# x taken transposed from the host as well: projections of the unnormalised x, the row scale rstd applied behind them

## The reference, cut to what matters

```python
def _rms_norm(x, gain):
    y = x * lax.rsqrt(jnp.mean(x * x, axis=-1, keepdims=True) + EPS)
    return y * gain

h = _rms_norm(x, norm_mix[l])
proj = h @ w_in[l]                                   # 1024 x 3072
q, k, v, cb, cc, cu = jnp.split(proj, splits, axis=-1)
q = _rms_norm(q.reshape(b, s, 8, 64), q_norm[l])     # k alike with k_norm
attn = stick_breaking_attention(q, k, v)             # strictly causal, 8 heads
conv = cb * causal_conv_width_3(cc * cu, conv_w[l])
x = x + concat([attn, conv]) @ w_out[l]
h = _rms_norm(x, norm_ffn[l])
x = x + (silu(h @ w_gate[l]) * (h @ w_up[l])) @ w_down[l]
```

## Time and profile before

| what | value |
|---|---|
| median of 3 runs | 2436.81 us (2435.79 to 2438.77) |
| the profiled execution | 2439.77 us, its span 2438.0 us, granted clock 0.999 |
| TensorE matmuls busy | 2405.6 us, 99% of the span |
| VectorE | 1456.5 us, 60% |
| ScalarE | 1165.8 us, 48% |
| GpSimd | 1240.2 us, 51% |
| DMA | 388.07 MB, mean 159 GB/s |

### The profile page before, as it was taken

The page is one execution under the profiler, slowest core; times in us unless marked ns, Lnnn a source line. Parts: engine busy times, 40 slices in busy tenths (PEclk is TensorE's granted clock), DMA queues, the critical chain, the costliest instruction groups (busy, mean ns, idle before and its releaser), DMA issues.

```text
span 2438.0 us, 33295 instructions
## 1 busy us (share of the span) xinstructions
PE 2405.6 (99%) x11880; PEld 2015.0 (83%) x11880; DVE 1456.5 (60%) x1499; ACT 1165.8 (48%) x1866; POOL 1240.2 (51%) x880
## 2 busy tenths in 40 slices
PE   8999999999999999999999999999999999999999
PEld 6888878888888888888888888888878888888887
DVE  4444377787777777436755555556645555554555
ACT  4322277788777777323533333334533333333333
POOL 1455367878787877104754544306755545440021
PEclk9999999999999999999999999999999999999999
DMA  6989874443634641534333233386743232325665
GB/s 199 312 286 289 253 222 108 143 113 101 176 84 120 175 132 54 172 130 165 124 112 125 78 116 110 124 291 224 230 150 110 88 125 78 116 95 193 223 218 199
DMA packets 337503, 388.07 MB, mean 159 GB/s; under 512 B 21472, under 2 KB 242784, under 8 KB 335072
## 3 DMA queue, kind: packets, MB, share of 16 engines
q1 hardware_dynamic: 337376, 386.49, 50.3%
HBM read 263.20 MB, written 123.21 MB: 158 GB/s over the span
## 4 chain that ended last, share of the span: by engine, by line
PE 90%; DVE 2%; DMA 2%; SPq 2%; issue 2%; ACT 1%; POOL 1%; ACTq 0%; DVEq 0%; POOLq 0%
PE lay_ps L2582 11%; PE lay_ps L2584 11%; PE lay_ps L2586 11%; PE lay_ps L106 8%; PE lay_ps L107 8%; PE lay_ps L108 8%; PE lay_ps L2612 5%; PE lay_ps L2613 5%; PE lay_ps L2614 5%; PE lay_ps L1381 5%; PE lay_ps L1369 2%; PE lay_ps L1388 2%; PE lay_ps L1368 2%; PE lay_ps L1387 2%; POOL lay_A L2486 1%
## 5 line engine op out<-in xcount | busy, mean ns | idle before, releaser
L2486 POOL TENSOR_TENSOR lay_A<-lay_raw,lay_A 128x512 fp32r<-128x512 f32 x264 | 365.0, 1395 | 376.1 <-ACT lay_A L2101 375.9
L2582 PE MATMUL lay_ps<-lay_B,lay_A 128*128 128x512 f32 x1232 | 479.6, 389 | 0.4 <-DVE lay_B_over L1741 0.2
L2584 PE MATMUL lay_ps<-lay_B,lay_A 128*128 128x512 f32 x1232 | 479.3, 389 | 0.0
L2586 PE MATMUL lay_ps<-lay_B,lay_A 128*128 128x512 f32 x1232 | 479.3, 389 | 0.0
L1288 POOL TENSOR_TENSOR lay_a<-lay_a,lay_stick 128x128 f32<-128x128 f32 (+5 forms) x192 | 282.4, 1478 | 105.1 <-DVE lay_stick L1229 48.3
L2351 DVE TENSOR_TENSOR lay_A<-lay_A_over,lay_A 128x1024 fp32r<-128x1024 f32 x154 | 215.9, 1403 | 163.9 <-ACT lay_A L2145 163.5
L2101 ACT ACTIVATE lay_A<-lay_raw 128x512 fp32r<-128x512 f32 x264 | 162.0, 627 | 282.9 <-DMA lay_raw<-in_w_gate 110.2
L2145 ACT ACTIVATE lay_A<-lay_A_over 128x1024 fp32r<-128x1024 f32 x154 | 163.1, 1060 | 242.5 <-PE lay_ps L2614 214.5
L2582 PEld LDWEIGHTS lay_ps<-lay_B,lay_A 128*128 128x128 f32 x1232 | 231.3, 188 | 49.3 <-POOL lay_A L2486 1.0
L2586 PEld LDWEIGHTS lay_ps<-lay_B,lay_A 128*128 128x128 f32 x1232 | 231.3, 188 | 47.9
L2584 PEld LDWEIGHTS lay_ps<-lay_B,lay_A 128*128 128x128 f32 x1232 | 231.3, 188 | 47.8
(11 more groups left out here) (145 smaller groups left out, 4979.5 us busy)
## 6 DMA issues: line engine op xcount, KB each, us to landing
hid_ops<-lay_s SPq DMA_DIRECT2D x154, 256.0 KB, 2.0
lay_A_over<-hid_ops SPq DMA_DIRECT2D x154, 256.0 KB, 2.8
lay_w_stage<-in_w_in SPq DMA_DIRECT2D x48, 512.0 KB, 4.8
lay_raw<-in_w_gate SPq DMA_DIRECT2D x22, 1024.0 KB, 5.6
lay_raw<-in_w_up SPq DMA_DIRECT2D x22, 1024.0 KB, 8.1
lay_A_over<-wd_ops SPq DMA_DIRECT2D x88, 256.0 KB, 3.0
lay_A_over<-in_w_down SPq DMA_DIRECT2D x66, 256.0 KB, 4.6
lay_wd_raw<-in_w_down SPq DMA_DIRECT2D x11, 1024.0 KB, 6.8
```

The costliest lines, as they stand in the source:

```text
L2486: nc.gpsimd.tensor_tensor(A[:, j, p, 1, :, :], operand(j, p), A[:, j, p, 0, :, :].bitcast(F32), ALU.subtract).then_inc(lo_done, 1)
L2582: nc.tensor.matmul(ps[:, b, :], A[:, j, p, 0, k, :], B[p][:, 0, k, :], start=first_mm, stop=False, skip_group_check=True)
L2584: nc.tensor.matmul(ps[:, b, :], A[:, j, p, 0, k, :], B[p][:, 1, k, :], start=False, stop=False, skip_group_check=True)
L2586: mm = nc.tensor.matmul(ps[:, b, :], A[:, j, p, 1, k, :], B[p][:, 0, k, :], start=False, stop=last_mm, skip_group_check=True)
```

## The change

The host hands over three more arrays, made by transposing alone: `x_columns` (x transposed, 1024 by 2048), `x_tiles` (the same, tile by tile, so that a tile is one contiguous 512 KB block) and `mix_gain` (the gain as 128 by 8, 4 KB). Since the row scale rstd of a token multiplies a whole row of h, it is left out of the projections' operand and put in afterwards.

- **Opening.** `x_transpose`, `x_norm` and both hT stores go. SyncE loads `x_tiles` (`load_xT`, 512 KB) beside the rows of x, which still serve `x_square`. VectorE multiplies the two halves by the gain in place (`gain_part`), ScalarE rounds (`hT_part`), VectorE makes the remainder, both now from SBUF. The order of the w_in thirds, of x and of xT at the start is new. The last two k steps of tiles 0 and 1 are done tile by tile. All loops over tiles are written out. rstd is used in the split of v (ScalarE with a scale, VectorE scalar_tensor_tensor). q and k are normalised per head, so their rstd falls out except beside eps: GpSimd makes eps_x = eps * msq and adds that in place of eps. SyncE stores rstd (`store_r`, 512 bytes).
- **Attention.** Row i of pair p is loaded raw from `x_columns` (`load_raw`, one DMA of 256 KB, 5 buffers), ScalarE multiplies by the gain and rounds (`row_hi`), VectorE makes the remainder (`row_lo`). The tables ROW_LOADS, ROW_HI and ROW_LO place them: five loads in units 8 to 17 of the pair before, three in 46 and 47; the splits behind the work of units 45 and 47 and of units 0 to 2 of the pair itself, on VectorE behind the scan of the unit. NU is 48, and n + NU is unit n of the pair itself. For the first pair five rows are loaded at tile 6 and split within tile 15, three follow the last q/k split. rstd of the 512 tokens is read as a broadcast row (`load_r`), squared by GpSimd once per pair (`square_r`, unit 4), multiplied into C*u (`times_r2`) and, as rstd, into the convolution's result before the gate (`scale_conv`): two more GpSimd operations for each of the 16 convolution tiles.
- COUNT for pairs 1 to 3 moves one step each: unit 2 from 0 to 1, unit 3 from 3 to 4, unit 4 from 2 to 0, units 42 and 43 from 1, 3 to 2, 2. The taps come two units behind the block in place of one.

```diff
+            def load_xT(t):
+                wait(sp, hT_lo_done, NB * (t - 1))
+                sp.dma_start(xT[:, t % 2, :, :].rearrange("p k t -> p (k t)"), x_tiles[t, :, :]).then_inc(xT_in[t % 2], DMA)
...
-            load_x(0, 0)
-            sp.dma_start(gain[:, :], norm_mix.partition_broadcast(P)).then_inc(gain_in, DMA)
-            load_x(1, 1)
+            load_xT(0)
+            load_w_third(0)
+            sp.dma_start(gain[:, :], gain_cols).then_inc(gain_in, DMA)
+            load_w_third(1)
+            load_xT(1)
+            load_w_third(2)
+            for k in range(1, KT):
+                if k == 2:
...
+                    load_x(0)
+                if k == 3:
+                    load_xT(2)
+                if k == 4:
+                    load_x(1)
...
+                nc.gpsimd.tensor_tensor(eps_x[:, b:b + 1], msq[:, b:b + 1], cst["eps"][:, 0:1],
+                                        ALU.mult).then_inc(eps_done, 1)
...
-                nc.vector.scalar_tensor_tensor(out=xn[:, b, :], in0=x_t[:, b, :], scalar=rstd[:, b:b + 1],
-                                               in1=gain[:, :], op0=ALU.mult, op1=ALU.mult).then_inc(xn_done, 1)
+            def gain_part(t, n):
+                dve.wait_ge(xT_in[t % 2], DMA * (t // 2 + 1))
+                part = xT[:, t % 2, 4 * n:4 * n + 4, :]
+                nc.vector.tensor_tensor(part, part, gain[:, 4 * n:4 * n + 4].unsqueeze(2).to_broadcast([P, 4, P]),
+                                        ALU.mult).then_inc(xg_done, 1)
...
                 project(t, 0)
-                if not last and not prepared(t + 1):
-                    x_transpose(t + 1, 1 - b, 0)
                 qk_transpose(t - 1, 0)
                 project(t, 1)
                 qk_transpose(t - 1, 1)
-                if not last and not prepared(t + 1):
-                    x_transpose(t + 1, 1 - b, 1)
                 project(t, 2)
...
+    ROW_LOADS = {8: [0], 9: [1], 10: [2], 16: [3], 17: [4], 46: [5], 47: [6, 7]}
+    ROW_HI = {NU - 3: [0, 1], NU - 1: [2, 3], NU: [4], NU + 1: [5, 6], NU + 2: [7]}
+    ROW_LO = {NU - 1: [0, 1], NU: [2, 3], NU + 1: [4], NU + 2: [5, 6, 7]}
...
-            def load_hT(p, i):
...
+            def load_raw(p, i):
+                n = KT * p + i
+                wait(sp, row_done, n - RAW + 1)
+                sp.dma_start(raw[:, n % RAW, :], xT[i * P:(i + 1) * P, p * BANK:(p + 1) * BANK]).then_inc(raw_in[n % RAW], DMA)
...
+            def row_hi(p, i):
+                n = KT * p + i
+                act.wait_ge(raw_in[n % RAW], DMA * (n // RAW) + DMA)
+                if is_first(p):
+                    act.wait_ge(opening.proj_full, 3 * (TILES - 1) + 1)
+                elif i < KT - 1:
+                    act.wait_ge(hT_used, (KT - 1) * (p - 1) + i + 1)
+                else:
+                    act.wait_ge(proj_full, NPROJ * p)
+                nc.scalar.activation(hT_hi[:, i, :], raw[:, (KT * p + i) % RAW, :], ACT.Copy,
+                                     scale=gain[:, i:i + 1]).then_inc(row_hi_done, 1)
...
+            def row_lo(p, i):
+                dve.wait_ge(row_hi_done, KT * p + i + 1)
+                nc.vector.scalar_tensor_tensor(out=hT_lo[:, i, :], in0=raw[:, (KT * p + i) % RAW, :],
+                                               scalar=gain[:, i:i + 1], in1=hT_hi[:, i, :].bitcast(F32),
+                                               op0=ALU.mult, op1=ALU.subtract).then_inc(row_done, 1)
...
+                nc.gpsimd.tensor_tensor(cu[:, HALO:HALO + BANK], cu[:, HALO:HALO + BANK], r_square[:, :],
+                                        ALU.mult).then_inc(cu_done, 1)
...
+                nc.gpsimd.tensor_tensor(conv[:, :], conv[:, :], r_row[:, :], ALU.mult).then_inc(conv_scaled, 1)
...
                 if k == 0:
-                    pe.wait_ge(hT_in[i], 2 * DMA * p + 2 * DMA)
+                    pe.wait_ge(row_done, KT * p + i + 1)
```

More of the change, by code:

```diff
@@ L350, in qkv_stage @@
         PIECES, FIRST_PIECE = w_down.shape[0] // (2 * P), 2
[L352 to L362 removed]
+        EARLY_ROWS = 6
         def w_count(k):
@@ L674, in step @@
[L674 to L684 removed]
+                if t == 1:
+                    qk_sums(1)
+                    v_part(1)
+                    for n in range(NB):
+                        gain_part(3, n)
+                    for n in range(NB):
+                        hT_part(3, n)
+                        qkT_part(0, n)
+                    qk_norm(1)
+                    return
```

676 lines of the change are left out of this document (342 added, 334 removed).

## The result

The changed kernel takes 2502.93 us (median of 4 runs, 2500.89 to 2505.63), 1.0271 times the kernel before (95% interval 1.0253 to 1.0288): 66 us slower, where 6.4 us faster was forecast.

A forecast was written before the change was run, and what follows sets the result against it. TensorE, busy 99% of the span, was taken to bound the kernel. The terms -14.7 - 4.4 + 12.0 + 0.7 = -6.4 us gave a forecast of 2430.4 us, range 2418 to 2444 (the forecast's own 2424 to 2437).

The forecast's parts named there:

- Part A and B: Opening and start: dropping x's transposes, an earlier start and fewer waits gain 14.7 us (12 to 17.5).
- 1.9 + 1.4 + 2 x 0.88: Opening: 1.9 us from the start, 1.1 and 0.3 of waits gone, two transpose groups of 0.44 saved per tile.
- a 512-byte store of rstd ... this stays hidden: Opening, per tile: the added loads, store and VectorE work stay hidden, with VectorE at 8 of 20 us.
- Rival 4: Opening: another engine or SyncE's queue takes over and a tile gets no shorter; +5.0, 2441.8 us; chance 0.07.
- Part C: Hand-over to attention: fewer waits for hT rows and v, and no clock dip; 4.4 us gained (1 to 5).
- The terms of the clock and of v: Hand-over: the 1.9 us wait for v disappears, and with it the clock dip over 318 to 338, 1.8 us.
- waits for the first scans: Hand-over: first scan late by about 1.8 us; scores 2 and 3 wait about 0.9 and 1.4 for it.
- Part D: Three boundaries between pairs: row splits on VectorE make TensorE wait, 4.0 us each, 12.0 lost.
- I take 0 (up to 1 per pair): Attention: GpSimd's two added multiplications per convolution tile, about 1.1 us each, cost TensorE nothing, up to 1 us per pair.
- rival 3: Pair boundaries: rows as forecast but the clock falls at each, 3 x 5.8 = 17.4; -1.0, 2435.8 us; chance 0.20.
- Rival 2: Pair boundaries: rows at 1.74 us cost 9.5, clock 1.8 more, 3 x 11.3; +15.5, 2452.3 us; chance 0.13.
- The end: End of attention: last y 2.4 later, GpSimd works beside the splitting of w_out; 0.7 us lost (0 to 2).

The follow-up runs named there:

- e1b: Changed kernel with an rstd column for each of the 16 tiles, so GpSimd no longer waits for the store two tiles back: 2456.59 us, 1.0081 times the kernel before.
- e6: As e1b, but in tile 14's step SyncE stores tile 13's q and k before issuing attention's k and q loads: 2449.51 us.
- e10: As e6, but rstd is transposed once in tile 15 and stored by one DMA of 16 rows instead of tile by tile: 2450.99 us.
- e3b: As e1b, with both added GpSimd multiplications per convolution tile narrowed from 512 columns to 8: 2438.3 us.
- e4b: As e1b, with VectorE's row remainder narrowed from 512 columns to 8 in all pairs but the first: 2447.9 us.
- e9: As e6, with ScalarE's and VectorE's row splits outside the first pair and both GpSimd multiplications narrowed to 8 columns: 2431.62 us.
- e12: As e10, but rows of h are stored hi and lo and loaded by DMA, and GpSimd's convolution work moves to other units: 2438.68 us.
- e13: As e10, row splits kept, with GpSimd's taps, scaling and gate of the convolution moved to other units: 2443.15 us.

## Why the prediction was wrong, step by step

**Part A and B, forecast -14.7, measured +27.8.** The sum came right: with the ring open (e1b) a tile takes 17.29 us instead of 18.13 and the opening ends at 290.9 instead of 305.5, a gain of 14.6; TensorE's first projection is at 8.55, a little outside the forecast 9.0 to 12.0. In part it is luck: by the start of tile 4 the gain is 7.2 (89.2 to 82.0), where the terms give 1.9 + 1.4 + 2 x 0.88 = 5.1, and from there on 7.4, where they give 9.7; one tile of e1b, the eleventh, takes 19.15. What failed is the clause "a 512-byte store of rstd ... this stays hidden". It was costed by its bytes, and the wait that comes with it was not named: `x_rstd` now waits for the landing of a store two tiles back, and queued behind that on GpSimd is the w_down piece, behind that SyncE, behind that the next store. Had the forecast named what is queued behind that wait and who waits for it, as it did for SyncE in unit 47, the ring would have shown itself without any duration. The store's length could only have been bounded: no transfer in the rows of before writes four-byte elements. Rival 4 named the mechanism, SyncE's queue taking over the opening, but priced it as a tile that gets no shorter; it got 3.5 us longer (18.1 to 21.6).

**Part C, forecast -4.4, measured +5.7 and +0.9.** The step that failed is again order: the forecast names SyncE's loads at the hand-over and leaves out tile 13's q/k store, which stands behind 12.6 us of them, while ScalarE's split of tile 15 waits for it. The stores of rstd made SyncE late (e6, e10), and the store had 5 us where it had 18. With the order mended (e6, e10), hand-over and first pair together take 169.3 and 168.2 us instead of 169.0, a gain of up to 0.8. The terms of the clock and of v did come back: over the 36 us from the first projection of attention the granted clock is 1.00 in both, 0.95 in the kernel before, and TensorE's wait for v is 0.8 in e6 and gone in e10. Its waits for the first scans, which the forecast had at 2.3, are 2.2 and 2.0. What is missing lies behind them: the first pair has the products too, which the forecast put at 0, and with them narrowed (e3b) the two together take 166.9, 2.1 less than before. The other 2.3 of the 4.4 were not found.

**Part D, forecast +12.0, measured +26.9** (9.3 + 9.3 + 8.3). The row's size was right: 1.15 forecast, 9.9 us for eight measured. TensorE's waits for rows came to 3.6, inside "3 to 5 us in all", and VectorE's remainders cost 4.0 a pair (e4b; 0.8 of it by the clock), the figure forecast for the rows. Two terms beside them failed: GpSimd's products, "I take 0 (up to 1 per pair)", cost 2.4 to 3.3, and 2.9 stay when all the added work is narrow (e9), where the forecast had waits and altered counts inside its 4.0. The clock fell at each boundary, as rival 3 said; it is worth 0.8 (e6), not 1.8, and does not always fall. Rival 2's 11.3 a boundary was nearer than the forecast's 4.0, but by luck: its premise (1.74 us a split) was wrong, the measured mean is 1.23, and it has nothing for the products. With the opening of e1b and the rest as measured the sum is -14.6 + 5.7 + 0.9 + 26.9 = +18.9, and e1b measured 1.0081, which is +19.7: the change is a loss even without the ring.

**The end, forecast +0.7, measured -0.1 to +1.6** (after; e1b).

## What to carry to other kernels

A new wait is priced by walking the ring it closes: what its engine has queued behind it, who waits for that, and whether the thing waited for is issued behind that. A store is priced by its elements as well as its bytes, and a queue that it fills makes the engine that issues late, so what must land early is issued before what need not (e6). Where engines are 71 to 85% busy, the place of added work (e12, e13: 2 to 4 us a pair) counts as its amount does (e3b: 2.4 to 3.3).

## What the runs showed of the hardware

- A DMA that writes 128 elements of 4 bytes from 128 partitions to DRAM takes 7.5 to 18.7 us to land in the ten kernels that do it, with medians of 10.9 to 16.0, and holds up what is issued around it: v's store 12.2 us with it and 3.4 without, x's load 10.4 and 4.7 (e6, e10). The Trainium skill, DMA: Bandwidth & Descriptors, Specifications, asks for 512 bytes or more at line rate and says that below this the engines read, modify and write; the direction agrees, and the size, 3.6 us of all 16 engines for 512 bytes, is this case's.
- A scalar_tensor_tensor of 512 columns with two SBUF inputs takes 739 to 750 ns while no GpSimd instruction runs, and 774 to 2114, 1668 in the median, while one runs for 95% of the time or more (kernel after).
- The same waits of TensorE do not always bring the clock down. 1.44 and 0.48 us, a group of three matmuls between them, came before a fall to half at the first two boundaries of the kernel after and of e1b; the same two, 1.45 and 0.48, at the three boundaries of e6 and the third of e1b before none.
